# A token mixer on one core: side work spread over more and later steps of the matmul stream, and a convolution that reads its accumulator where it lies

## What is computed

```python
proj = hn @ w_in                       # split into q, k, v, g_out, g_low, z, xbc, dt, gate_a, gate_b
o = gla_chunked(q * dk**-0.5, k, v, log_g)            # gated linear attention: chunks of 64, 4 heads
o = rmsnorm(o, gla_norm_w) * silu(g_out)
y_a = o @ w_up_gla
xbc = silu(causal_dwconv(xbc, conv_w, conv_b))        # four taps along the tokens
xs, Bm, Cm = split(xbc)
y = ssd_chunked(xs * dt, a, Bm, Cm) + d_skip * xs     # 4 groups of 8 heads
y = rmsnorm(y * silu(z)) ; y_b = y @ w_up_ssd
mixed = sigmoid(gate_a) * y_a + sigmoid(gate_b) * y_b
out = mixed @ w_out
```

## Time and profile before

| | us |
|---|---|
| median of 3 runs | 1598.37 |
| lowest and highest run | 1596.96 and 1599.61 |
| the profiled execution's own time | 1598.98 |
| its span, first to last instruction | 1597.1 |

### The profile page before, as it was taken

How to read it: one execution, slowest core, us unless ns; L and a number is a source line. 1 busy time by engine, 2 the same in 40 slices (tenths; PEclk the granted TensorE clock), 3 DMA queues, 4 the chain that set the end, 5 groups by cost and what they waited for, 6 DMA issues and landing times. The chain is left out here.

```text
span 1597.1 us, 19058 instructions
## 1 busy us (share of the span) xinstructions
PE 1390.8 (87%) x6585; PEld 997.3 (62%) x6585; DVE 1086.7 (68%) x2077; ACT 735.5 (46%) x1270; POOL 297.6 (19%) x260
## 2 busy tenths in 40 slices
PE   6998978899999788877877878678799999999997
PEld 6987978787989433333333333233398688998776
DVE  5767467875668777777777777675687466765664
ACT  5665777747455322222222222221354466656772
POOL 0000000000003555444544445443100000000000
PEclk9999989999999899898989889999999999999999
DMA  6353444444567999999999999999755456454542
GB/s 227 125 181 87 152 133 132 146 132 156 176 206 299 420 421 420 422 421 421 421 422 421 422 420 422 421 421 421 309 176 173 132 173 196 152 176 135 151 138 81
DMA packets 77808, 417.73 MB, mean 262 GB/s; under 512 B 8768, under 2 KB 8832, under 8 KB 44688
## 3 DMA queue, kind: packets, MB, share of 16 engines
q0 software_dynamic: 36864, 268.45, 40.4%
q1 hardware_dynamic: 40848, 148.06, 29.1%
HBM read 415.39 MB, written 1.08 MB: 261 GB/s over the span
## 5 line engine op out<-in xcount | busy, mean ns | idle before, releaser
L321 PE MATMUL ps<-AR 128*128 128x512 f32 (+6 forms) x1164 | 362.0, 462 | 94.1 <-ACT AR L1213 68.0
L222 DVE TENSOR_TENSOR wlo<-raw,whi 128x1024 fp32r<-128x1024 f32 x257 | 311.6, 1221 | 154.1 <-ACT whi L221 153.4
L321 PEld LDWEIGHTS ps<-AR 128*128 128x128 f32 (+2 forms) x1164 | 190.1, 196 | 257.5 <-issue 127.5
L221 ACT ACTIVATE whi<-raw 128x1024 fp32r<-128x1024 f32 x257 | 269.3, 1054 | 121.3 <-PE ps L260 99.6
L321 PE MATMUL ps<-SLAB,AR 128*128 128x512 f32 x516 | 258.0, 656 | 62.8 <-ACT AR L1213 62.6
L260 PE MATMUL ps<-XH,whi 128*128 128x256 f32 (+1 forms) x1032 | 306.4, 297 | 4.7 <-DVE XL L332 2.4
L260 PE MATMUL ps<-XL,whi 128*128 128x256 f32 (+1 forms) x1032 | 296.7, 288 | 0.0
L260 PE MATMUL ps<-XH,wlo 128*128 128x256 f32 (+1 forms) x1032 | 296.6, 287 | 0.0
L1178 POOL DMA_INDIRECT AR<-in_peer_uv,C x127 | 151.6, 1194 | 654.6 <-DVE C L1132 487.9
L321 PEld LDWEIGHTS ps<-SLAB,AR 128*128 128x128 f32 x516 | 105.2, 208 | 211.0 <-issue 126.3
L260 PEld LDWEIGHTS ps<-XH,whi 128*128 128x128 f32 x1032 | 200.4, 194 | 13.5 <-DVE XL L332 5.5
(11 more groups left out here) (253 smaller groups left out, 1237.7 us busy)
## 6 DMA issues: line engine op xcount, KB each, us to landing
raw<-in_stream SPq DMA_DIRECT2D x257, 512.0 KB, 3.7
AR<-scr SPq DMA_DIRECT2D x8, 512.0 KB, 5.1
SLAB<-in_peer_uv,C POOLq DMA_INDIRECT x129, 28.1
AR<-in_rows SPq DMA_DIRECT2D x4, 512.0 KB, 4.7
AR<-in_peer_uv,C POOLq DMA_INDIRECT x127, 27.4
AR<-in_con SPq DMA_DIRECT2D x1, 1280.0 KB, 7.1
AR<-in_xin SPq DMA_DIRECT2D x2, 512.0 KB, 5.0
AR<-in_xin SPq DMA_DIRECT2D x1, 1024.0 KB, 8.0
```

Source lines behind the costliest of these rows:

```text
L221: a = A(lambda e: e.activation(h[:, :], r, ACT.Copy), loaded[i], free, chain=False)
L222: b = V(lambda e: e.tensor_tensor(l[:, :], r, h[:, :].bitcast(F32), ALU.subtract), a, loaded[i], free, chain=False)
L321: return PE(lambda e: e.matmul(out_ap, l, r, start=start, stop=stop, skip_group_check=onto), *after, signal=sig)
```

## The change

The yields between stages of `gla_side`, `ssd_side` and `y_side` are increased (one of four to three, for the last y), and from the fourth x tile to the end of z the stream makes three steps a chunk in place of two; T tiles get their third step at k == 5. After z, `until("yT7")` has the first two groups of y emitted before the third begins. In `conv`, the buffer `XP` and the copy into it go: DVE reads the earlier tokens from the PSUM bank itself (`o[:, 0:T - n]`) and adds them to the later columns of `dst`. `use` returns the last DVE token, so that the bank comes free after it and no longer after ACT's fourth tap.

```diff
--- before.py
+++ after.py
@@ -287,6 +287,8 @@
                                 while mid:
                                     mid.pop(0)()
                                 side_step(2)
+                            if k == 5:
+                                side_step(3)
                         used[i] = tok
                         if kg == kt - 1:
                             bank_free[b] = use(o, tok)
@@ -600,8 +602,8 @@
             prod = V(lambda e: e.tensor_tensor(chunked(qS[:, :, :], 1), qE1[:, :, :, :],
                                                chunked(GX[:, :, X], 0)[:, :, :, 63:64].broadcast_to([128, 4, 2, 64]), ALU.mult))
             att_zero = V(lambda e: e.memset(attS[64:128, :, :, 0:64], 0.0))
-            yield
-            yield
+            for _ in range(4):
+                yield
 
             def features(i, v):
                 for g in range(2):
@@ -664,8 +669,8 @@
                 bank_free[5] = bank_free[6] = v
                 if i == 0:
                     held = features(i, v)
-            yield
-            yield
+            for _ in range(5):
+                yield
             yield from features(1, v)
 
 
@@ -685,7 +690,6 @@
 
         BT = place("BT", 22224, 4 * T).rearrange("p (g t) -> p g t", g=4)
         CT = place("CT", 23312, 4 * T).rearrange("p (g t) -> p g t", g=4)
-        XP = place("XP", 24400, 552).rearrange("p (b t) -> p b t", b=2)
         XSG = place("XSG", 24952, 2176).rearrange("p (b f t) -> p b f t", b=2, f=4)
         GA = place("GA", 7120, 2048).rearrange("p (f t) -> p f t", f=8)
         GB = place("GB", 9168, 2048).rearrange("p (f t) -> p f t", f=8)
@@ -699,9 +703,7 @@
         IN = place("IN", 20432, 512)
         ZS = place("ZS", 20944, 1024).rearrange("p (b c) -> p b c", b=2)
 
-        xp_free = [None, None]
         cbm_zero = None
-        v0 = V(lambda e: e.memset(XP[:, :, 0:3], 0.0), x_ready)
 
         late = []
 
@@ -714,16 +716,15 @@
         def conv(f, dst, first_free):
 
             def use(o, tok):
-                p = f % 2
-                a = A(lambda e: e.copy(XP[:, p, 3:3 + T], o), tok, xp_free[p], v0)
                 w = P_CONVW + 4 * f
-                a = d = A(lambda e: e.activation(dst, o, ACT.Identity, bias=par_(P_CONVB + f), scale=par_(w + 3)), first_free())
+                d = A(lambda e: e.activation(dst, o, ACT.Identity, bias=par_(P_CONVB + f), scale=par_(w + 3)), tok, first_free())
                 for j in range(3):
-                    v = V(lambda e, j=j: e.scalar_tensor_tensor(dst, XP[:, p, j:j + T], par_(w + j), dst, ALU.mult, ALU.add), d)
-                xp_free[p] = v
+                    late_by = 3 - j
+                    v = V(lambda e, j=j, n=late_by: e.scalar_tensor_tensor(dst[:, n:T], o[:, 0:T - n], par_(w + j), dst[:, n:T],
+                                                                           ALU.mult, ALU.add), d)
                 silu()
                 late.append((f, dst, v))
-                return a
+                return v
             return use
 
         def cons_gate(dst, key):
@@ -783,8 +784,8 @@
         def ssd_side(g):
             x = XSG[:, g % 2, :, :]
             Mg = M[:, g % 2, :, :, :]
-            yield
-            yield
+            for _ in range(5 if g else 8):
+                yield
             silu()
             cs = [pts[f"c{4 * g + j}"] for j in range(4)]
 
@@ -871,6 +877,7 @@
                     until(f"xsg{f // 4 - 2}")
                 r = inner(o, tok)
                 if f % 4 == 3:
+                    ring["steps"] = 3
                     sides.append(ssd_side(f // 4))
                 return r
             return use
@@ -918,7 +925,7 @@
             yield
             while g > 1 and "z_done" not in pts:
                 yield
-            for _ in range(4 if g == 3 else 2):
+            for _ in range(3):
                 yield
             for j in range(4):
                 f = 4 * g + j
@@ -932,6 +939,7 @@
 
         stream_N(4, 8, 0, T, NM, x_ready, use_z)
         pts["z_done"] = PE.now()
+        until("yT7")
         last = y_side(3)
         next(last)
         sides.append(last)
@@ -968,6 +976,7 @@
                 yield
 
         sides.append(mix_side())
+        ring["steps"] = 2
         stream_T([(0, TX, cons_yb(f)) for f in range(8)], y_at, TX, yt_ready)
         side_all()
         mix_features()
```

## The result

The changed kernel takes 1585.45 us (median of 4 runs, 1585.1 to 1588.28) beside 1597.89 of the kernel before on the same chip: a ratio of 0.9925, 95% interval 0.9908 to 0.9942, which is 12.4 us less.

A forecast was written before the change was run, and what follows sets the result against it. PE bounds the kernel (267 of 300 us busy); its waits and low clock could give back at most 42.1. Savings 11.8 + 10.4 + 4.7 + 0.3 = 27.2 us; 1598.98 - 27.2 - 0.6 = 1571.2, stated as 1571.5, range 1558 to 1586.

The forecast's parts named there:

- its last part: Signs expected in the profile after: waits at tile 19 or 20, 3 us for the first turn's product, near 3 for y's diagonals.
- Attention: Attention and the heads' norm: waits of 8.9 us shrink to 0.5 at `prod`; with two low-clock stretches, 11.8 us saved.
- Group 0: Group 0's turns and first state: new PE waits of 2.2, 1.4, 3.05 and 0.6 us, together 7.3, bounds 0 and 11.
- Clock: ... I take none.: Groups 0 and 1: no clock fall behind the new waits; bound two stretches of 3.4 us at half, 3.4.
- Group 3's first state waits 0.2: At group 3's first state, counted under y: PE waits 0.2 us.
- After that DVE ... catches up: After group 0's waits, DVE catches up, with 4 us of splits and taps per 5.9 us pair of tiles.
- groups 1 to 3 have two chunks between `load_bc` and Abs, 6 us or more against 5.9: Later groups' rows of decays: 6 us or more from load to first Abs, against 5.9 measured before the change.
- In the run of six x tiles DVE has 24.6 us of work and PE 26.4 ... 0.5 left, bounds 0 and 3: Group 2 and its first state: waits of 5.2 us shrink to 0.5, net 4.7, as DVE has less work than PE.
- Y: The two y groups: waits of 0.3 and 3.2 us, low clock behind the second; net 0.3 with group 3, bounds -1 and 6.9.
- the lag is worse and the clock falls with it: Rival, chance 0.18: 10.4 us less gain at group 0, group 2 and `prod`; 1582 us, up to 1586 if `features` waits.
- the rules of the Trainium skill against the edit: Conv: copy matmul output to SBUF before many operations; PSUM access costs DVE about 65 ns more, 4.7 us for 72 taps.

The follow-up runs named there:

- e2: The changed kernel with the old conv (copy into `XP`, bank freed by ACT), so the steps alone: 1587.19 us, 0.9931 of the kernel before.
- e6: e3 with the halves of `M` swapped, so that group 0's rows of decays also load early, at the start of the gate and x tiles: 1575.89 us, 0.9861.
- e10: e6 with group 0's Abs and Exp spread over the steps behind `attention(1)` and its rows loaded at `prod`: 1562.86 us, 0.9783.
- e9: The changed kernel with four products that nobody reads put before group 3's first state: 1583.60 us, 0.9921.
- e3: The changed kernel with the loads of decay rows for groups 1 to 3 moved to the first turn of the group before: 1581.06 us, 0.9896.
- e13: e10 with five empty steps put back in front of group 0: 1570.94 us, 0.9819.
- e11: The changed kernel without two of the three DVE taps of x tiles 8 to 13, which changes the output: 1577.98 us, 0.9889.
- e1: The kernel before with the new conv alone, no step moved: 1595.34 us, 0.9983.
- e14: e6 with group 0's Abs left where they were but in one step, later stages five steps sooner: 1569.63 us, 0.9813.
- e7: e6 with two more steps before the second y group: 1575.83 us, 0.9868.

## Why the prediction was right in its sign and wrong in its size

The mechanism was right: the waits for Silu and the heads' norm went, DVE's taps cost nothing more from PSUM, and the places that its last part named are there: tiles 19 and 20, the first turn's product, y's diagonals with the low clock behind them. What failed is that it let DVE catch up behind group 0 and gave the later groups' loads too much room. The terms, left over as predicted and as measured:

- **Attention.** `prod` 0.5, measured 0.77. Not foreseen: 0.72 for the V product, which now waits behind it, and 1.02 at a transpose (L326) for DVE's `XL`. Together 2.0 too little.
- **Group 0.** 2.2, 1.4, 3.05 and 0.6, measured 1.84 and 1.52 (tiles 18 and 19), 1.29, 2.92 and none: 7.6 for 7.3. The chain worked out from rows held; e2, e6 and e10 show its parts (ACT waiting for the rows, then 16 Abs and an Exp in two and a half tiles). That the sum fits so closely is partly luck: ACT stood 3.97 us for the rows, not 2.6, tile 18's wait was not foreseen, and the last wait did not come.
- **"Clock: ... I take none."** That step failed: the clock fell after 2.92, 6.41 us of work at half speed, 3.2 lost, the bound that was given for it.
- **"Group 3's first state waits 0.2"**, and **"After that DVE ... catches up; groups 1 to 3 have two chunks between `load_bc` and Abs, 6 us or more against 5.9"**. This step failed worst: 4.54 us and 3.45 of clock, 7.8 too little. The two chunks do not count from the issue: the load is queued behind group 2's first state, which PE made at 295.63, but SP issued it at 300.62, behind a load of weights. The prediction counted such a delay, 1.1 us, for group 0 alone. ACT was free 3.9 us after the issue, not 6. With 5.9 us it would have stood 2.0, as it did in e2 (2.20) and e9 (2.30). The rest is that the rows took 8.7 us in this one execution; how much of the median that explains is open. e3 takes the wait away by loading earlier.
- **"After that DVE ... catches up"** for group 1, and **"In the run of six x tiles DVE has 24.6 us of work and PE 26.4 ... 0.5 left, bounds 0 and 3"** for group 2. Group 2 waits for nothing; group 1, for which nothing was counted, now falls into that run and waits 2.99 for `XE`, with 1.7 of clock: together 4.2 too little. DVE did not catch up, and a balance over the whole run of six x tiles hid the order within it: the product stands behind two tiles' taps (e13), and with fewer taps it is not late (e11).
- **Y.** 0.3 and 3.2, measured 0.38 and 2.68; the clock fell, but over 3.16 us of work and not 5.8. 1.8 too much. The terms named for the second wait (8.6, four times 0.5 and 1.05) add up to 11.65 and not 11.9, so 2.95 would have stood there.

2.0 + 0.3 + 3.2 + 7.8 + 4.2 - 1.8 = 15.7: the 27.2 of the sum become 11.5, beside 12.43 at the mixer's end and 12.4 between the medians. The rival "the lag is worse and the clock falls with it" came near the time, at 1582 to 1586, by luck: it put 7 us more at group 0 and 2.5 at group 2, where the runs show 3.5 more at group 0 (7.6 and 3.2 of clock for 7.3), nothing at group 2, and most of the rest at groups 1 and 3. On the rules of the Trainium skill against the edit, e1 is the test: the conv alone is 1.4 us faster, and the rows of 497 to 500 ns from PSUM stand against the 65 ns that the Trainium skill (Perfetto Trace Analysis, Optimizing Scalar/DVE Operations) would add.

What the runs show beyond this: three causes remained in the changed kernel, rows of decays that come late (e3 and e6), ACT's work of group 0 in too few tiles (e10), and stages that come five steps too late (e14). Removing all three, as e10 does, gives 1562.86 us, some 22 below the changed kernel. Not settled: why y waits at one place of the stream and not at the other was not followed row by row, and of e10's 36.7 us in the mixer (411.21 to 374.55) 34.2 show in the time; where the rest stays behind the mixer was not looked for.

## What to carry to other kernels

When yields are added between a producer and its reader, write down where every later stage lands, and what the helper engines have in their queues there; a balance of busy time over the stretch hides a wait of 3 us. Work that needs only early data (here Abs and Exp of the decays) is better moved into an emptier stretch than given more steps: that shortened the list and freed the stages behind it. For a load queued behind others, count from where its engine will really issue it to where its reader is free (3.9 us here, not 6), and price it from its slowest landing. Give each forecast wait near 2 us or more its chance of a low clock.

## What the runs showed of the hardware

After a wait of PE the clock fell or it did not, for waits of the same length at the same place: `XE`'s 2.99 us was followed by 0.50 in the changed kernel, e3 and e13 and by no fall in e6, e7 and e9; the 2.37 of `features` by none in e10, the 2.38 in e13 by 3.4 us of it; the place of the 4.54 us, filled with unread products, by none (e9). Length alone did not decide: 1.72 us in e2 was followed by 3.4 us of it, 3.57 us in e1 by none. Where ACT stood waiting for them, the rows of decays took 6.45, 5.89 and 8.70 us from issue to the first Abs at groups 0, 2 and 3 of the changed kernel, and 5.98 at group 3 in e9; why was not followed. A 128x512 product took 1.04 us on GpSimd and 0.69 on DVE.
